# A two-block network on one core: the low part of thirteen weight units of the even layer's input projection on GpSimd instead of VectorE

## What is computed

```python
def even_layer(x, mem_n, cos, sin, norm_g, w_in, gate_b, pe_k, w1_k, w2_k, pe_v, w1_v, w2_v, w_mem_kv, w_out):
    h = rms_norm_2(x, norm_g)
    (nq, nkc, nvc, nks, nvs, nkw, nvw, ng, nz, mq, mk, mv, mz, eq, ez) = _split(h @ w_in, EVEN_SPLITS)
...
    kc = nsa_compress(rot(nkc), pe_k, w1_k, w2_k)
    vc = nsa_compress(heads(nvc), pe_v, w1_v, w2_v)
    gates = jax.nn.sigmoid(ng + gate_b).reshape(Bsz, T, NSA_BRANCHES, NSA_HEADS)
    a_out = nsa_attention(rot(nq), kc, vc, rot(nks), heads(nvs), rot(nkw), heads(nvw), gates)
    b_out = moba_attention(rot(mq), rot(mk), heads(mv))
    m_out = memory_attention(heads(eq), mem_n, w_mem_kv)
    y = jnp.concatenate([a_out * jax.nn.silu(nz), b_out * jax.nn.silu(mz),
                         m_out * jax.nn.silu(ez)], axis=-1) @ w_out
    return x + y
```

## Time and profile before

| | |
|---|---|
| Median of 3 runs | 2298.92 us (2298.03 to 2300.6) |
| The profiled execution | 2300.05 us |
| Its span, first to last instruction | 2298.2 us |
| Mean granted TensorE clock over the span | 0.999 |
| TensorE busy | 2281.4 us, 99% |
| VectorE busy | 1677.7 us, 73% |
| ScalarE busy | 1404.6 us, 61% |
| GpSimd busy | 181.4 us, 8% |
| HBM read | 394.54 MB, 172 GB/s over the span |
| The stage of the change on TensorE's timeline | 1876.1 to 2035.9 us |

### The profile page before, as it was taken

One profiled execution on the slowest core, in us unless ns is written; L12 is line 12 of the kernel. 1 busy time (PEld: TensorE's weight loads), 2 busy tenths in 40 slices (PEclk: granted clock), 3 DMA queues, 4 the chain that ended last, 5 costly groups with the idle time before them and its releaser, 6 DMA issues.

```text
span 2298.2 us, 42511 instructions
## 1 busy us (share of the span) xinstructions
PE 2281.4 (99%) x14253; PEld 1996.9 (87%) x14253; DVE 1677.7 (73%) x3045; ACT 1404.6 (61%) x2618; POOL 181.4 (8%) x257
## 2 busy tenths in 40 slices
PE   9999999999999999999999999999999999999998
PEld 8799999999888888999899999988888888788777
DVE  6767997999655555775999799966555668767565
ACT  5657666888544455446666788844555555665554
POOL 1002121111000000000211211100000010000000
PEclk9999999999999999999999999999999999999999
DMA  7455666444566666566566544466666654346454
GB/s 244 146 185 163 187 183 181 142 144 141 184 193 193 195 192 192 177 183 192 168 182 190 166 141 146 147 207 192 191 211 181 194 187 136 86 139 197 131 165 146
DMA packets 137470, 397.50 MB, mean 173 GB/s; under 512 B 12480, under 2 KB 13808, under 8 KB 136560
## 3 DMA queue, kind: packets, MB, share of 16 engines
q1 hardware_dynamic: 134448, 384.71, 54.9%
q0 software_dynamic: 2448, 10.56, 1.4%
q10 hardware_dynamic: 432, 0.36, 0.0%
HBM read 394.54 MB, written 1.05 MB: 172 GB/s over the span
## 4 chain that ended last, share of the span: by engine, by line
PE 92%; DVE 5%; issue 1%; ACT 1%; DVEq 0%; POOLq 0%; POOL 0%; ACTq 0%
PE bank L1176 29%; PE bank L1148 13%; PE bank L1004 13%; PE bank L1160 11%; PE bank L1010 7%; PE bank L1152 7%; PE bank L1189 4%; DVE wl L2000 2%; PE bank L1036 1%; PE bank L1252 1%; PE bank L1104 1%; PE bank L1128 1%; PE bank L1015 0%; DVE aux L2038 0%; PE bank L1080 0%
## 5 line engine op out<-in xcount | busy, mean ns | idle before, releaser
L2000 DVE TENSOR_TENSOR wl<-raw,wh 128x1024 fp32r<-128x1024 f32 x726 | 886.8, 1223 | 501.2 <-ACT wh L1525 488.3
L1525 ACT ACTIVATE wh<-raw 128x1024 fp32r<-128x1024 f32 x725 | 764.4, 1055 | 602.2 <-PE bank L1176 327.7
L1148 PE MATMUL bank<-x_both,wh 128*128 128x512 f32 x1328 | 337.4, 396 | 0.0
L1148 PEld LDWEIGHTS bank<-x_both,wh 128*128 128x128 f32 x1328 | 238.2, 189 | 42.7
L1176 PE MATMUL bank<-wh,gl 128*128 128x512 f32 x992 | 265.6, 389 | 0.0
L1176 PE MATMUL bank<-wh,gh 128*128 128x512 f32 x992 | 265.3, 389 | 0.0
L1176 PE MATMUL bank<-wl,gh 128*128 128x512 f32 x992 | 265.2, 389 | 0.0
L1176 PEld LDWEIGHTS bank<-wh,gl 128*128 128x128 f32 x992 | 185.9, 188 | 39.5 <-DVE gl L2349 1.0
L1176 PEld LDWEIGHTS bank<-wl,gh 128*128 128x128 f32 x992 | 186.2, 188 | 38.8
L1176 PEld LDWEIGHTS bank<-wh,gh 128*128 128x128 f32 x992 | 186.0, 188 | 38.4
L1004 PE MATMUL bank<-wh,x_both 128*128 128x512 f32 (+1 forms) x768 | 195.9, 397 | 0.2 <-DVE x_both L2046 0.2
(11 more groups left out here) (334 smaller groups left out, 2876.8 us busy)
## 6 DMA issues: line engine op xcount, KB each, us to landing
raw<-in_w_upT SPq DMA_DIRECT2D x256, 512.0 KB, 3.6
raw<-in_w_down SPq DMA_DIRECT2D x256, 512.0 KB, 3.7
raw<-in_l_w_in SPq DMA_DIRECT2D x84, 512.0 KB, 3.7
raw<-in_peer_w_query SPq DMA_DIRECT2D x32, 512.0 KB, 3.8
raw<-in_l_w_out SPq DMA_DIRECT2D x28, 512.0 KB, 3.7
raw<-in_conv_w_in SPq DMA_DIRECT2D x24, 512.0 KB, 3.8
raw<-in_attn_w_qkv SPq DMA_DIRECT2D x23, 512.0 KB, 4.6
arena<-in_na_bias POOLq DMA_DIRECT2D x4, 1024.0 KB, 6.2
```

The source lines that it names most:

```text
L1148: pe.matmul(banks[b].rearrange("p (a b) -> p a b", a=2), lhsT=w[0][:, k, :], rhs=x_both[:, :, k, :], start=k == 0, stop=False, skip_group_ ...
L1525: act.activation(unit_parts(n)[0][:, 0:kts * cols], raw[:, n % RAW, 0:kts * cols], ACT.Copy)\
L2000: tt(lo[:, 0:kts * cols], raw[:, n % RAW, 0:kts * cols], hi[:, 0:kts * cols].bitcast(F32), ALU.subtract)\
```

## The change

The low parts of units 9, 11, 13, ... 33 of the stage (13 units) are made by GpSimd with the same subtraction on the same buffers. GpSimd waits for `hi_ready` of the unit and raises a semaphore of its own, `even_low`. TensorE waits for that one before the low matmuls of these units. VectorE skips them; before the low part of the next unit it waits for `even_low` of the skipped one and raises `lo_ready` in its place by a no-op, so that the counter still rises in order, and SyncE's next load follows from that.

```diff
--- before.py
+++ after.py
@@ -201,6 +201,7 @@
 EVEN_YT = (0, 1, 4, 2, 3)
 EV_AT = (16, 18, 20, 21, 22, 23, 24, 25, 26, 27, 28, 29, 30, 31)
 EV_T, EV_O = 2, 3
+EVEN_POOL = range(9, 35, 2)
 
 
 def even_pairs(n, lag=0):
@@ -526,6 +527,8 @@
         half_done = sem("down_first_half_done")
         landed = [sem(f"raw{s}_landed") for s in range(RAW)]
         hi_ready, lo_ready = sem("unit_high_ready"), sem("unit_low_ready")
+        even_lows = {first_unit["even_in"] + u: k + 1 for k, u in enumerate(EVEN_POOL)}
+        even_low = sem("even_unit_low_by_gpsimd")
         units_used = sem("units_used")
         x_whole, x_high, x_low = sem("x_whole"), sem("x_high"), sem("x_low")
         extra_loaded = {n: sem(f"{n}_loaded") for n in ("bias0", "bias1", "bias2", "bias3", "keys", "cmpw", "decay", "gain", "mem", "masks", "lanes")}
@@ -873,6 +876,12 @@
             for kv in "kv":
                 pool.dma_start(w1[kv], d[f"w1_{kv}"]).then_inc(extra_loaded["cmpw"], 16)
             dump("between")
+            for n in even_lows:
+                kts, cols = units[n][1:]
+                pool.wait_ge(hi_ready, n + 1)
+                hi, lo = unit_parts(n)
+                pool.tensor_tensor(lo[:, 0:kts * cols], raw[:, n % RAW, 0:kts * cols], hi[:, 0:kts * cols].bitcast(F32),
+                                   ALU.subtract).then_inc(even_low, 1)
             row_scales("odd")
             pool.dma_start(decay, d["c_decay"]).then_inc(extra_loaded["decay"], 16)
             pool.dma_start(gain_bc, d["final_norm"].partition_broadcast(P)).then_inc(extra_loaded["gain"], 16)
@@ -988,7 +997,9 @@
                         for part in range(2):
                             if part:
                                 middle(k0 // UKT)
-                            if n or part:
+                            if part and n in even_lows:
+                                pe.wait_ge(even_low, even_lows[n])
+                            elif n or part:
                                 pe.wait_ge((hi_ready, lo_ready)[part], n + 1)
                             for kk in range(UKT):
                                 kt = k0 + kk
@@ -1994,6 +2005,11 @@
 
             def low(n, i=0):
 
+                if n in even_lows:
+                    return
+                if n - 1 in even_lows:
+                    dve.wait_ge(even_low, even_lows[n - 1])
+                    dve.nop().then_inc(lo_ready, 1)
                 kts, cols = (1, UNIT) if units[n] is None else units[n][1:]
                 dve.wait_ge(hi_ready, unit_wait(n + 1, i))
                 hi, lo = unit_parts(n)
```

## The result

The changed kernel takes 2304.34 us in the median of 11 runs (2304.09 to 2306.84); the kernel before, on the same chip, 2298.25 (2297.91 to 2300.6, 11 runs). The ratio is 1.0026, with a 95% interval of 1.0019 to 1.0034: slower by 6.1 us, where 6.0 was forecast. The profiled execution took 2304.34 us with a span of 2302.5.

A forecast was written before the change was run, and what follows sets the result against it. TensorE bounds the kernel, but VectorE's queue sets the pace from about 1925 to 1958. Six steps of TensorE lateness sum to 6.0 us: 2306.1 us profiled, 1.13 less for the median, 2304.9 us; range 2297.0 to 2309.0.

The forecast's parts named there:

- GpSimd's price: One GpSimd subtraction of 128x1024 takes 2.39 us, of 128x560 1.40 us, extrapolated from additions; VectorE's takes 1.23 us.
- The hold: A GpSimd subtraction shuts out VectorE operations with both inputs in SBUF for about 2.35 us; those reading PSUM pass.
- Step 1: Unit 11: GpSimd's 1.40 us block falls on the rope of 1905.65, which has 1.03 us slack; TensorE +0.3 us.
- Step 2: Units 13 and 15: gate bias addition, then the rope from 1917.94 are held; TensorE, wanting it at 1920.78, +1.9 us.
- Steps 3 and 4: Unit 17: VectorE, spared a subtraction, takes compressed scores less late, -0.3 us; unit 19: softmax products at 1937.79 held, +1.1.
- Steps 5 and 6: Unit 21: rope at 1946.77 held, +1.1 us; unit 23: gate product at 1955.16 held, row maxima behind it, +1.9.
- The low clock stretch: Eight matmuls after TensorE's second gap at the lower clock, costing some 1.5 us; taken to come once, as before.
- The load queue: Loads are told of a moved unit only at VectorE's next one; no cost, 2.5 us of cover left.
- No hold: Rival, chance 0.13: long GpSimd operations let VectorE through, second gap starts TensorE 1.7 us earlier; 2297.2 to 2295.7 us.
- Cheap places: Rival, chance 0.18: GpSimd gets the port only during VectorE's PSUM operations, later holds nearly vanish; 2300.8 to 2303 us.
- Blocks of 2.97 us: Rival, chance 0.12 with a second low clock stretch: longer GpSimd operations add 3.1 us, 2308.0; the stretch too, 2309.5.
- The gap of 4 to 5 us near 1962: Sign that the forecast is right: one TensorE gap of 4 to 5 us near 1962, the stretch after 1966 as before.

The follow-up runs named there:

- E6: The changed kernel with only units 25, 27, 29, 31 and 33 moved to GpSimd; 2298.6 us, ratio 0.9999.
- E1: The changed kernel with GpSimd filling the thirteen low parts with zeros, about as long, instead of subtracting, all waits kept; 2298.93 us, ratio 0.9996.
- E3: The kernel before, plus same-size GpSimd subtractions on a spare buffer at the thirteen moments, nobody waiting for them; 2304.58 us, ratio 1.0025.
- E2: The changed kernel with VectorE making all low parts again, the change's waits, no-ops and late signals kept; 2300.1 us, ratio 1.0004.
- E7: The changed kernel with each of the thirteen GpSimd subtractions split into four pieces of a quarter of the columns; 2301.52 us, ratio 1.001.
- E8: The changed kernel with only units 17, 18, 20 and 22 moved, GpSimd also waiting for rope (18) and softmax (20); 2297.06 us, again 2296.79.

## Why the prediction was right, point by point

1. **What bounds the kernel**: right. All of the loss up to the restart arose at TensorE's waits between 1905 and 1966, and units 25 to 33 cost nothing (E6, 0.0 by lowest times).
2. **GpSimd's price**: right, 2.39 us taken from additions of 2 and 256 elements, 2387 ns measured; 1.40 and 1.39 for 560. The estimate of 2.25 us, half of what the Trainium skill gives for 2048 elements (GPSIMD Engine Reference, section 3.1), was 0.14 too low at 1024 elements.
3. **The hold**: right, and shown from three sides. Without GpSimd's reads the loss is gone (E1), with nobody waiting for GpSimd it is there (E3), with all the waits and no GpSimd it is not (E2). What the Trainium skill says (SBUF — State Buffer, "Who interferes with whom"), that a VectorE instruction with two SBUF inputs contends with a GpSimd one that reads SBUF and that whichever issues first has the shared port pair for its whole instruction, agrees with the trace down to an operation of 0.16 us (E3: 1.33 us), with E1 and with E7.
4. **Step 1** (+0.3): right in size, hidden in the number. The rope was held for 1.2 us, and TensorE, 0.20 ahead of the execution before at its previous step (1907.57 for 1907.77), was 0.03 behind it after: a loss of 0.23.
5. **Step 2** (+1.9): 1.64, from 0.03 to 1.67. The gate bias addition ended at 1915.19, forecast 1915.3; GpSimd's second block at 1921.40, forecast 1921.6.
6. **Steps 3 and 4** (-0.3, +1.1; together +0.8): 2.41 - 1.67 = 0.74. The place was another: step 4 had the softmax products held, and it was the second half of the rope before them, from 1936.99, so that TensorE had a new gap of 1.32 us at 1940.10 for `roped`, and the gap before the scores shrank from 0.87 to 0.58.
7. **Steps 5 and 6** (+1.1, +1.9; together +3.0): 5.54 - 2.41 = 3.13. In step 6 GpSimd got in between the halves of the rope, at 1957.65, and not before the gate product; the block is as long wherever it falls.
8. **The low clock stretch** ("to come once, as before"): the step that failed. In the profiled execution the eight matmuls after the second gap ran at full clock, and the low level came before the last gap, which took it up, as the rows of 1961.68 and 1963.44 show, so that the lateness went from 5.54 back to 4.3 at the end of the span (2302.5 against 2298.2). The profile should have come to 2306.1 and came to 2304.34. That the median was still met within 0.6 us is partly luck: the prediction put the median 1.13 us under the profiled execution, and for the changed kernel they are the same, which nearly makes up for the first error. The sum itself was good without that luck: 5.73 up to the restart and 6.2 by lowest times, against 6.0.
9. **The load queue at no cost**: right as far as tested; E2 has its signals with VectorE's own work and loses 0.3 us in the trace, all of it at two waits of VectorE. **The no-ops**, put at under 0.1 us each and at nothing in the sum, were sized too small: 0.15 each with their wait, and those of units 18 and 22 reach TensorE.
10. **The rivals.** "No hold" fell, and its price was too high too: E1 has no hold and wins 0.6 to 1.0 us, not 1.7 to 3.2. Of its 1.68 us earlier on VectorE, 1.26 are left when three waits of 0.14 (units 18, 20 and 22) are taken off, and E1's trace shows 1.30 (the last maxima at 1955.52 for 1957.07, less the 0.25 by which that execution was ahead from the start of the stage). The upper end had also counted the low clock as the gap's doing; E1's second gap is 2.07 us, and the clock after it 1.00. "Cheap places" did not occur by itself; in E8 GpSimd was given waits of its own to bring it about. Blocks of 2.97 us did not come. The gap of 4 to 5 us near 1962, named as a sign, came as two, 2.55 and 0.94.

## What to carry to other kernels

Before work goes from VectorE to an idle GpSimd, ask what VectorE will be doing at that moment: an instruction with both inputs in SBUF stands still until GpSimd's has ended, and one of 0.2 us lost 1.3 here. In this kernel the offload paid, by little, only where VectorE's queue set the pace and had work from PSUM beside it, and GpSimd's own waits placed it there; shorter GpSimd instructions made each hold shorter. Idle percentages show none of this. And where effects are of one or two microseconds and the times fall into groups, compare group with group, and the stage itself between two marks of the trace, not only medians.

## What was not expected of the hardware

- A GpSimd fill that reads nothing leaves the rope's two-input operations alone (E1), but not every one-input operation. VectorE's timeline of E1, during the fills of 1912.55 to 1915.11; the second row takes 0.18 us undisturbed:

```profile
1913.51 0.21 DVE L2676 TENSOR_TENSOR arena<-arena,gate_b 128x48 f32<-128x48 f32 x1 [3.49 <-ACT arena L1525]
1913.75 0.81 DVE L2667 TENSOR_SCALAR aux<-aux 64x60 f32<-64x60 f32 x1
```

  It ends at 1914.56, and the second fill at 1914.52. Beside E7's subtractions the same step takes 0.64 us. So two inputs in SBUF is not the whole list of what is held.

- A GpSimd subtraction of 128x1024 with one tile as both inputs takes 1.90 us (E3), with two tiles 2.39. Whether the shared tile or the output type makes it is open.
- The lower clock level came in some executions and not in others with the same gaps on TensorE (E6 against before, and E8 against itself). What decides it stays open here; no run changed it by itself.
